# Three scans side by side: outputs and new states taken one unit later, side products moved behind the second products of each level, states updated from the bank in blocks

## The chip, the cores and the metric

One core of one Trainium2 chip. The time is the device time of one execution in microseconds, the median of three runs. All data are float32.

## The reference, cut to what matters

Two layers of a hybrid model over 256 context tokens and 256 latent tokens of width 1024. In each layer the normed tokens are projected, and the columns feed three groups of recurrences, each run forwards and backwards in chunks: a state space model (SSD, 8 heads, state 128), a gated linear recurrence (HGRN2, 4 heads of 64) and a gated delta rule (GDN, 4 heads of 64). Then come an output projection and a mixture of 64 experts. Only the recurrences are touched:

```python
# SSD:   h_t = exp(da_t) h_{t-1} + B_t (x_t dt_t)^T,         y_t = h_t C_t
# HGRN2: S_t = diag(f_t) S_{t-1} + k_t v_t^T,                o_t = S_t^T q_t
# GDN:   M_t = exp(g_t) (I - b_t k_t k_t^T) M_{t-1} + b_t k_t v_t^T,   o_t = M_t^T q_t
# GDN by chunk:
lhs = a_strict + jnp.eye(CHUNK)
sol = lax.linalg.triangular_solve(lhs, rhs, left_side=True, lower=True, unit_diagonal=True)
v_new = u_c - w_c @ s
o = qg_c @ s + qk_c @ v_new
s = d_c * s + ke_c^T @ v_new
```

Every latent scan starts from the last context state of its direction. In layer 1 the context tokens' outputs are not needed any more, only their states.

## The kernel before, in words

**Stages.** Per layer: norms, input projection, convolutions, then the scans, then output projection and experts (weights of 1 MB blocks stream in). The scans work on chunks of 128 tokens, four of them (two of context, two latent), in two directions: eight units (`UNITS`), alternating between the directions. A unit is live (`wanted` in the code) when its chunk's outputs are needed: all eight in layer 0, the last four in layer 1. `outs(l, u)` counts live units up to u. The first unit that visits a chunk (`SEEN`) writes the outputs `yraw`, the second adds to them.

**The chain in a unit.** The delta rule's triangular system is inverted by doubling in seven levels (j = 0 to 6), for four heads in two halves. At each level PE waits for a masked matrix from GpSimd (`masked`, line 643, semaphore `nt_ready`) and for the inverse so far from VectorE (`t_ready`), and makes the level's *first products* (4 matmuls, semaphore `p_ps`). ScalarE copies them out of the bank (line 807, `p_sb`). Then PE makes the level's *second products* with them (8 matmuls, at the last level 4, `q_ps`), and VectorE subtracts them from the inverse (`w_next`, through the helper at line 1064). Level 0 has first products only (`w_first`). A float32 matmul stands in the trace as two matmul records.

**The rest of the work in a unit** is placed by hand between these steps, in four in-order queues:
- PE: `decays` (cumulative decays as products with a triangle), `key_products`, `h_products` (HGRN's products of levels, four steps of 8 matmuls), the products with the delta state (`gks_ps`), and for the unit before `values` (new values of the delta rule), `ssd_outputs` and `ends` (delta outputs and new states).
- VectorE: for the unit before `hgrn_state`, `ssd_out`, `gdn_end`, `ssd_state`; for this one `gdn_rhs` (right-hand side), the HGRN keys at the chunk's end (`kend`), `h_levels` (masked copies of the level products out of the bank, its drain at line 1342 raises `h_cp`), score weighting of SSD, `hgrn_out`; for the next one `hgrn_scans`, `hgrn_levels`, `keys` and `queries` (line 1292; their drains at lines 1299 and 1304 raise `at_ready`). The drain at line 1385 ends `ssd_state`. Most operations are followed by a drain.
- ScalarE: the copies of first products, `levels_exp` (absolute value and exponential of 1792 columns, for HGRN's levels, semaphore `hexp`), `vn_copy` (the new values), the exponential of the space model's decays, decay steps (line 933).
- GpSimd: the seven masks of a unit, the products of HGRN's level factors with keys and queries (line 651), SSD's weighted inputs `xw` and `xdt`, the delta keys `kw`.

**Placement before.** PE puts `values` and `ssd_outputs` of the unit before between levels 0 and 1, `ends` after level 1's second products. Decays and key products of the next unit stand between the first and second products of levels 2 and 3; the last two steps of `h_products` stand between those of levels 4 and 5, behind a wait for `h_cp`; HGRN's output and new state between those of level 6. A state update of HGRN or of the delta rule multiplies the bank by a block mask `bd` into `tmp` and then does one scalar_tensor_tensor for each of two tiles of 128 columns; SSD's state is scaled in one operation and added to in another.

Of the kernel before, what the change touches and what calls it, by code (L numbers as in the profile page):

```python
# [147 lines left out]
def build(nc, A, out, scratch):  # L148
    f_dram, acc_dram, acc_odd, tab_dram = scratch
    with ExitStack() as ctx:  # L150
# [184 lines left out]
        for name, n in (  # L335
# [17 lines left out]
            ("ke_ps", U - 2), ("ke_sb", U - 2), ("ho_ps", U), ("hgrn_done", U),  # L353
            ("ssd_pre", U), ("e_ssd", U), ("cb_ps", U), ("att_ready", U), ("kw_ready", U), ("ssd_ps", U), ("ssd_sb", 2 * U),
# [235 lines left out]
        def _(pool):  # L590
# [36 lines left out]
            for l in range(DEPTH):  # L627
# [32 lines left out]
                for u, (i, d, c) in enumerate(UNITS):  # L660
                    wanted, un = c in LIVE[l], outs(l, u)
                    if wanted:
                        if u:
# [19 lines left out]
                    if wanted:  # L683
                        do(G.tensor_tensor(by_head(xdt[:, :]), xs(c), heads(dt_[:, c, d, 0:HS]), ALU.mult))
                    pool.drain().then_inc(S["kw_ready"], 1)
                    masked(u, 5)
                    masked(u, 6)
                    if u + 1 < U:
# [106 lines left out]
        def _(act):  # L795
# [41 lines left out]
            for l in range(DEPTH):  # L837
# [84 lines left out]
                def levels_exp(u):  # L922
                    wait("b_ready", u + 1, l)
                    if UNITS[u][2] in LIVE[l]:
                        f(e7[:, :, :], e7[:, :, :], ACT.Abs)
                        f(e7[:, :, :], e7[:, :, :], ACT.Exp, scale=-1.0)
# [13 lines left out]
                def vn_copy(u):  # L940
                    wait("vn_ps", u + 1, l)
                    f(vn[:, :], ps[:, 4, 0:HW], ACT.Identity, "vn_sb")
# [3 lines left out]
                levels_exp(0)  # L946
                e_gdn(0)
                for u, (i, _, c) in enumerate(UNITS):
                    wanted, un = c in LIVE[l], outs(l, u)
                    if u:  # L950
                        vn_copy(u - 1)
                        wait("ho_ps", u, l)
# [4 lines left out]
                    for j in range(1, LEVELS):  # L957
# [5 lines left out]
                        if j == 2:  # L963
# [3 lines left out]
                            if u + 1 < U:  # L967
                                e_gdn(u + 1)
                        if j == 5:
                            if wanted:  # L970
                                wait("ssd_pre", un, l)
                                f(E[:, :, :].rearrange("p h t -> p (h t)"), bank(6, 2), ACT.Exp, "e_ssd")
                            if i < NT - 1:
                                wait("ke_ps", u + 1, l)
                                f(kendT[:, :], ps[:, 5, 0:2 * P], ACT.Identity, "ke_sb")
                    if u + 1 < U:
                        levels_exp(u + 1)
# [74 lines left out]
        def _(dve):  # L1052
# [91 lines left out]
            for l in range(DEPTH):  # L1144
# [199 lines left out]
                def hgrn_out(u):  # L1344
                    _, _, c = UNITS[u]
                    if c in live:
                        wait("ho_ps", u + 1, l)
# [5 lines left out]

                def hgrn_state(u):
                    i, d, _ = UNITS[u]
                    if i < NT - 1:
                        wait("ho_ps", u + 1, l)
# [20 lines left out]
                def ssd_state(u):  # L1378
                    i, d, c = UNITS[u]
                    if i < NT - 1:  # L1380
                        wait("go_ps", u + 1, l)
                        sv = Ss[:, d, :, :].rearrange("p g f -> p (g f)")
                        tt(by_head(sv), by_head(sv), heads(etot[:, c, d, 0:HS]), ALU.mult)
                        tt(sv, sv, ps[:, 7, :], ALU.add)
                    dve.drain().then_inc(S["ssd_sb"], 1)

                def gdn_rhs(u):
# [3 lines left out]
                    h4 = lambda ap: ap.rearrange("p (h v) -> p h v", h=HH)  # L1391
                    tt(h4(rr[:, :]), h4(ps[:, 4, 0:HW]), gdn(eacs[:, c, d, HS:NDEC]), ALU.mult)
                    o = yraw[:, c, SW + HW:DM]
                    if c in live:
# [791 lines left out]
```

## Time and profile before

| | us |
|---|---|
| median of three runs | 2959.13 |
| lowest and highest | 2950.36, 2961.5 |
| the profiled execution | 2956.34 |
| its span | 2954.6 |
| mean granted TensorE clock | 0.917 of full |

| engine | busy us | share of the span | instructions |
|---|---|---|---|
| PE (matmul) | 2497.5 | 85% | 14732 |
| DVE (VectorE) | 1199.4 | 41% | 2349 |
| ACT (ScalarE) | 631.6 | 21% | 1140 |
| POOL (GpSimd) | 667.9 | 23% | 686 |

The shares are averages over stages with different limits. The scans fill about 323 to 717 us (layer 0) and 1890 to 2195 us (layer 1) of the span. Rows of the trace name an engine, the line of kernel.py (often that of a helper), the tile written and those read, and how long the engine stood idle before it and what ended that. `R` is the big scratch tile, `ring` holds a part of the working tiles during the scans, `ps` is the eight banks of PSUM. "DVEq" is a signal of VectorE's queue (a drain or a semaphore instruction) rather than of one of its operations.

### The profile page before, as it was taken

How to read it: one execution, taken by the hardware profiler on the slowest of the kernel's cores; microseconds unless marked ns; L12 is line 12 of the kernel's file. 1: busy time of each engine (PE TensorE's matmuls, PEld its weight loads, DVE VectorE, ACT ScalarE, POOL GpSimd, SP SyncE). 2: the span in 40 equal slices, each digit the busy share in tenths (PEclk: the TensorE clock that was granted, in tenths of full speed). 3: DMA queues.
4: the chain of work that ended last, by engine and by line, in shares of the span. 5: the costliest groups of instructions: out<-in, count | busy, mean ns of one | idle time of the engine just before them, and what ended most of it. 6: DMA issues, size and time to landing. Idle time of an engine off the chain costs nothing.

```text
span 2954.6 us, 43826 instructions
## 1 busy us (share of the span) xinstructions
PE 2497.5 (85%) x14732; PEld 1683.9 (57%) x14733; DVE 1199.4 (41%) x2349; ACT 631.6 (21%) x1140; POOL 667.9 (23%) x686
## 2 busy tenths in 40 slices
PE   5999788886866989999997598898867798999995
PEld 2348677776733555555554245787766455555552
DVE  4532576766261222222221543477664222222223
ACT  1125332322010111111111114523230111111111
POOL 0000253532013222222221000235321222222221
PEclk8999788988878999999999799999788899999998
DMA  6634000001152999999996352200016499999994
GB/s 257 256 132 90 1 1 1 1 1 34 46 222 96 367 353 358 348 336 333 365 349 217 131 199 71 47 1 1 1 34 246 167 367 362 367 365 358 381 351 148
DMA packets 188878, 573.16 MB, mean 194 GB/s; under 512 B 56543, under 2 KB 99879, under 8 KB 149831
## 3 DMA queue, kind: packets, MB, share of 16 engines
q1 hardware_dynamic: 162150, 520.29, 47.2%
q0 software_dynamic: 26592, 51.11, 7.1%
q8 instruction: 81, 1.33, 0.2%
q14 instruction: 55, 0.44, 0.0%
HBM read 552.37 MB, written 53.53 MB: 205 GB/s over the span
## 4 chain that ended last, share of the span: by engine, by line
PE 61%; DVE 13%; DMA 13%; issue 6%; ACT 2%; DVEq 2%; POOLq 1%; another core or an unknown queue 1%; ACTq 1%; SPq 1%; POOL 0%
PE ps L1659 56%; DMA featT<-ffn_rows,idx_in 7%; PE ps L1663 5%; DVE R L1064 4%; DMA R<-in_exp_down 4%; DVE featT L1064 1%; ACT R L807 1%; DVE R L1337 1%; DVE ring L1064 1%; POOLq L723 1%; DMA R<-in_w_mod 1%; ACT L807 1%; DMA R<-ffn_sum_even 1%; DVEq L1061 1%
## 5 line engine op out<-in xcount | busy, mean ns | idle before, releaser
L1659 PE MATMUL ps<-R 128*64 128x256 f32 (+5 forms) x9040 | 1427.7, 385 | 112.1 <-issue 49.4
L1659 PEld LDWEIGHTS ps<-R 128*64 128x64 f32 (+2 forms) x9040 | 884.7, 168 | 521.9 <-issue 284.7
L807 ACT ACTIVATE R<-ps 128x256 f32<-128x256 f32 (+3 forms) x395 | 175.4, 444 | 1197.9 <-PE ps L1659 1052.5
L1064 DVE TENSOR_TENSOR R<-R,ps 128x256 f32<-128x256 f32 (+2 forms) x250 | 137.3, 549 | 564.1 <-ACT R L807 500.4
L1659 PE MATMUL ps<-featT,ring 128*128 128x512 f32 (+1 forms) x768 | 312.4, 564 | 1.1 <-ACT R L807 0.8
L1659 PE MATMUL ps<-ring,R 128*128 128x128 f32 (+2 forms) x1200 | 262.4, 355 | 35.9 <-DMA ring<-in_sh_down 20.1
L1659 PEld LDWEIGHTS ps<-ring,R 128*128 128x128 f32 x1200 | 209.3, 215 | 70.4 <-issue 47.0
L1663 PE MATMUL ps<-ident,featT 128*128 128x128 f32 x1120 | 163.3, 292 | 98.3 <-DMA featT<-ffn_rows,idx_in 59.6
L1659 PEld LDWEIGHTS ps<-featT,ring 128*128 128x128 f32 x768 | 147.9, 196 | 162.8 <-issue 156.1
L643 POOL TENSOR_TENSOR R<-ring,lev 128x512 f32<-128x512 f32 x56 | 73.9, 1319 | 680.6 <-DVEq L1299 292.9
L1067 DVE TENSOR_SCALAR R<-ps,idx_out 128x512 f32<-128x512 f32 x128 | 96.1, 751 | 300.4 <-PE ps L1659 300.4
L1663 PEld LDWEIGHTS ps<-ident,featT 128*128 128x128 f32 x1120 | 128.8, 148 | 154.3 <-issue 64.6
L747 POOL DMA_INDIRECT ffn_sum_even<-R,idx_out x64 | 93.8, 1466 | 499.8 <-issue 499.8
L1073 DVE COPY R<-ps 128x256 f32<-128x256 f32 (+2 forms) x282 | 154.5, 548 | 112.5 <-PE ps L1663 91.3
L747 POOL DMA_INDIRECT ffn_sum_odd<-R,idx_out x64 | 94.2, 1472 | 439.0 <-issue 439.0
L807 ACT ACTIVATE R<-ps,idx_out 128x512 f32<-128x512 f32 x128 | 88.0, 688 | 380.0 <-PE ps L1659 380.0
L716 POOL DMA_INDIRECT featT<-ffn_rows,idx_in x128 | 126.8, 991 | 54.3 <-issue 49.8
L1002 ACT ACTIVATE R<-ps 128x512 f32<-128x512 f32 x128 | 76.4, 597 | 234.0 <-PE ps L1663 228.3
L1064 DVE TENSOR_TENSOR R<-R 128x256 f32<-128x256 f32 (+5 forms) x116 | 95.2, 821 | 66.0 <-ACT R L807 56.6
L1659 PE MATMUL ps<-ring,featT 128*128 128x256 f32 x512 | 113.7, 382 | 1.0 <-issue 1.0
L643 POOL TENSOR_TENSOR R<-R,lev 128x512 f32<-128x512 f32 x56 | 75.2, 1343 | 164.9 <-PE ps L1659 153.3
L1659 PEld LDWEIGHTS ps<-ring,featT 128*128 128x128 f32 x512 | 97.8, 192 | 17.0 <-issue 4.0
(197 smaller groups left out, 1837.6 us busy)
## 6 DMA issues: line engine op xcount, KB each, us to landing
R<-in_exp_gate SPq DMA_DIRECT2D x128, 1024.0 KB
R<-in_exp_up SPq DMA_DIRECT2D x128, 1024.0 KB
R<-in_exp_down SPq DMA_DIRECT2D x128, 1024.0 KB
R<-in_w_mod SPq DMA_DIRECT2D x48, 1024.0 KB, 7.4
ring<-in_w_in SPq DMA_DIRECT2D x30, 1024.0 KB, 5.4
ring<-in_w_out SPq DMA_DIRECT2D x8, 1024.0 KB, 7.5
ffn_sum_odd<-zero SPq DMA_DIRECT2D x6, 512.0 KB, 8.4
ffn_rows<-X SPq DMA_DIRECT2D x6, 512.0 KB
```

The source lines that it names most:

```text
L643: do(G.tensor_tensor(NTm[:, run % 2, :, :], AT[u % 2][:, :, :], lev[:, UNITS[u][1], j, :].unsqueeze(1).to_broadcast([P, HH, P]), ALU.mult) ...
L716: pool.indirect_dma_start(xg[s][0:n, :], None, f_dram, bass.IndirectOffsetOnAxis(idxG[s][0:n, 0:1].bitcast(U32), 0), bounds_check=TOK - 1, ...
L723: wide = pool.value_load(more[0:1, at_], min_val=0, max_val=1)
L747: pool.indirect_dma_start((acc_dram, acc_odd)[s % 2], bass.IndirectOffsetOnAxis(idxS[s][0:n, 0:1].bitcast(U32), 0), oe[s % 2][0:n, :], Non ...
L807: do(C.activation(out_, in_, func, **kw), name)
L1002: do(C.activation(xgT[b][:, 0:4, :].rearrange("p k t -> p (k t)"), ps[:, 0, :], ACT.Identity), "xt_sb")
L1061: dve.drain()
L1064: do(V.tensor_tensor(out_, a, b, op), name)
L1067: do(V.tensor_scalar(out_, a, s1, s2, op0, *(() if op1 is None else (op1,))), name)
L1073: do(V.tensor_copy(out_, in_), name)
L1659: return MM(out_, lhsT, rhs, start=start, stop=stop)
L1663: return nc.tensor.transpose(out_, in_, ident[0:k, 0:k])
```

## The change

Semaphores `hs_ps` (HGRN's new state product) and `st_ps` (SSD's) are added, so that outputs and states signal apart. Where an order is changed, it is that of PE, VectorE, ScalarE and GpSimd; no DMA is added or moved. In PE's queue:
- level 0: after its products `values`, `h_state`, `ssd_scores` of the unit before; the values now go to bank 3.
- level 1: the products with the delta state wait for `hgrn_done` in place of `vn_sb`.
- level 2: `ssd_outputs` of the unit before between first and second products (it stood at level 0).
- level 3: next unit's decays between the products; then SSD's new state of the unit before (it was part of `ends`).
- level 4: key products of the next unit and step 2 of `h_products`, all behind the second products; level 5: step 3 and the eight SSD decays, likewise.
- level 6: transposes of `kend` between the products, HGRN's output `h_out` behind them.

```diff
 # GpSimd: xw after mask 6
-                    do(G.tensor_tensor(by_head(xw[:, :]), xs(c), heads(wdt[:, c, d, 0:HS]), ALU.mult))
...
                     masked(u, 6)
+                    if i < NT - 1:
+                        if u:
+                            wait("st_ps", u, l)
+                        do(G.tensor_tensor(by_head(xw[:, :]), xs(c), heads(wdt[:, c, d, 0:HS]), ALU.mult))
+                    pool.drain().then_inc(S["kw_ready"], 1)
 # ScalarE
                     if u:
                         vn_copy(u - 1)
-                        wait("ho_ps", u, l)
+                    levels_exp(u)
+                    if un > 1:
+                        wait("ho_ps", un - 1, l)
                     f(eb[:, :], bh[:, :], ACT.Exp, "eb_ready")
...
+                    if i < NT - 1:
+                        wait("ke_ps", u + 1, l)
+                        f(kendT[:, :], ps[:, 5, 0:2 * P], ACT.Identity, "ke_sb")
+                    if wanted:
+                        wait("ssd_pre", un, l)
+                        f(E[:, :, :].rearrange("p h t -> p (h t)"), bank(6, 2), ACT.Exp, "e_ssd")
                     if u + 1 < U:
-                        levels_exp(u + 1)
+                        levels_abs(u + 1)
 # VectorE: states
+                def add_blocks(state, keep, new):
+                    for t in range(2):
+                        for half in range(2):
+                            own = slice(half * HD, (half + 1) * HD)
+                            V.scalar_tensor_tensor(state[own, t, own], state[own, t, own], keep[own, t:t + 1],
+                                                   new[own, t * P + half * HD:t * P + (half + 1) * HD], ALU.mult, ALU.add)
...
-                        tt(tmp[:, 0:2 * P].rearrange("p (t v) -> p t v", t=2), ps[:, 5, 2 * P:4 * P].rearrange("p (t v) -> p t v", t=2),
-                           bd[:, :].unsqueeze(1).to_broadcast([P, 2, P]), ALU.mult)
-                        for t in range(2):
-                            V.scalar_tensor_tensor(Sh[:, d, t, :], Sh[:, d, t, :], hdec[:, t:t + 1], tmp[:, t * P:(t + 1) * P], ALU.mult, ALU.add)
+                        wait("hs_ps", u + 1, l)
+                        add_blocks(Sh[:, d, :, :], hdec[:, :], ps[:, 5, 2 * P:4 * P])
...
-                        tt(by_head(sv), by_head(sv), heads(etot[:, c, d, 0:HS]), ALU.mult)
-                        tt(sv, sv, ps[:, 7, :], ALU.add)
+                        for q in range(HS):
+                            own = slice(q * HD, (q + 1) * HD)
+                            V.scalar_tensor_tensor(sv[:, own], sv[:, own], etot[:, c, d, q:q + 1], ps[:, 7, own], ALU.mult, ALU.add)
...
+                def scores(u):
+                    _, d, c = UNITS[u]
+                    if c in live:
+                        wait("cb_ps", outs(l, u), l)
+                        wait("e_ssd", outs(l, u), l)
+                        g2 = ps[:, 6, 0:NG * P].rearrange("p (g t) -> p g t", g=NG)
+                        tt(g2, g2, tri[:, d, :].unsqueeze(1).to_broadcast([P, NG, P]), ALU.mult)
+                        e4 = E[:, :, :].rearrange("p (g r) t -> p g r t", g=NG)
+                        tt(e4, e4, g2.unsqueeze(2).to_broadcast([P, NG, HS // NG, P]), ALU.mult, "att_ready")
 # VectorE: right-hand side
-                    tt(h4(rr[:, :]), h4(ps[:, 4, 0:HW]), gdn(eacs[:, c, d, HS:NDEC]), ALU.mult)
...
-                        tt(h4(to), h4(ps[:, 4, HW:2 * HW]), gdn(eacs[:, c, d, HS:NDEC]), ALU.mult)
-                    r22 = rr[:, :].rearrange("p (a f) -> p a f", a=2)
-                    tt(r22, cv[:, 12:14, tk(c)], r22, ALU.subtract, "r_ready")
-                    if c in live and SEEN[c] != u:
-                        tt(o, o, tmp[:, 0:HW], ALU.add)
+                    for q in range(HH):
+                        own = slice(q * HD, (q + 1) * HD)
+                        by = eacs[:, c, d, HS + q:HS + q + 1]
+                        V.scalar_tensor_tensor(rr[:, own], ps[:, 4, own], by,
+                                               cv[:, 12 + q // 2, c * P + (q % 2) * HD:c * P + (q % 2 + 1) * HD], ALU.mult, ALU.subtract)
+                        if c in live and SEEN[c] != u:
+                            V.scalar_tensor_tensor(o[:, own], ps[:, 4, HW + q * HD:HW + (q + 1) * HD], by, o[:, own], ALU.mult, ALU.add)
 # PE: after the last unit
                 values(U - 1)
+                ssd_scores(U - 1)
+                ends(U - 1)
                 ssd_outputs(U - 1)
-                ends(U - 1)
```

The comment lines name the place of a hunk. `gdn_end` changes like `hgrn_state`, and `levels_abs` is the first operation of the old `levels_exp`.

VectorE's order in a unit before: `w_first`; `hgrn_state`, `ssd_out` of the unit before; `w_next` 1; `gdn_end` (before), `gdn_rhs`; `w_next` 2; `ssd_state` (before), `hdec`, `eb`, `kend`, scans of the next unit; then ahead of each `w_next` 3 to 6 a step of `h_levels` and some of the next unit's `hgrn_levels`, `keys` after `w_next` 3, `queries` after 4, score weighting and `hgrn_out` of the same unit ahead of `w_next` 6.

After: `w_first`; `hgrn_out`, `hgrn_state`, `scores` of the unit before; `w_next` 1; `gdn_end` (before), `gdn_rhs`, `kend`, `hdec`, `eb`; `w_next` 2; `ssd_out` (before), `h_levels` 0; `w_next` 3; `ssd_state` (before), the next unit's scans, `h_levels` 1, `hgrn_levels` 0 and 1; `w_next` 4; `keys`, `queries` (next), `h_levels` 2, `hgrn_levels` 2 and 3; `w_next` 5; `h_levels` 3, `hgrn_levels` 4 to 6; `w_next` 6.

## Rows read from the trace of the kernel before

**Rows 1.** The page's first line.

```profile
span 2954.6 us, 43826 instructions
```

**Rows 2.** Stretches: us; PE, PEld, DVE, ACT, POOL busy (instructions); PEclk, DMA share, GB/s.

```profile
323.28:716.70 393.42, 327.30 (x2520) 308.14 (x2519) 262.66 (x478) 113.67 (x242) 165.49 (x207) 0.86 0.02 7
617.50:667.30 49.80, 41.30 (x323) 39.05 (x322) 35.56 (x65) 14.72 (x32) 21.59 (x27) 0.86 0.01 1
1911.40:1938.30 26.90, 24.47 (x189) 22.17 (x188) 18.20 (x35) 8.13 (x22) 10.93 (x10) 1.00 0.01 2
1995.40:2194.80 199.40, 162.93 (x1262) 153.07 (x1261) 132.13 (x232) 59.47 (x124) 82.58 (x103) 0.87 0.04 13
```

**Rows 3.** Waits in layer 0's scans: who <- for whom: us, times, longest.

```profile
DVE ring L1064 <- PE ps L1659: 39.6, 28, 6.0
DVE R L1064 <- PE ps L1659: 39.3, 28, 5.9
...
PE ps L1659 <- DVEq L1342: 18.2, 12, 2.6
PE ps L1659 <- DVEq L1304: 14.8, 7, 2.1
...
PE ps L1663 <- DVEq L1342: 11.7, 6, 2.2
...
PE ps L1659 <- DVEq L1385: 9.3, 6, 1.9
DVE featT L1064 <- PE ps L1659: 6.8, 8, 1.5
...
DVE R L1292 <- PE ps L1659: 5.3, 4, 1.8
...
DVE featT L1073 <- PE ps L1659: 4.9, 4, 2.1
```

**Rows 4.** VectorE's operations by shape in layer 0's scans: count | busy, mean ns | idle before.

```profile
L1064 DVE TENSOR_TENSOR R<-R,ps 128x512 f32<-128x512 f32 x50 | 34.4, 687 | 34.5 <-PE ps L1659 32.1 <-issue 0.2
...
L1064 DVE TENSOR_TENSOR R<-R 128x256 f32<-128x256 f32 x24 | 17.7, 737 | 1.8
L1064 DVE TENSOR_TENSOR R<-R 128x1024 f32<-128x1024 f32 x8 | 12.6, 1580 | 0.7 <-issue 0.2
L1064 DVE TENSOR_TENSOR R<-R 128x512 f32<-128x512 f32 x6 | 8.9, 1489 | 0.6
...
L1064 DVE TENSOR_TENSOR featT<-featT,R 128x256 f32<-128x256 f32 x4 | 5.4, 1361 | 0.4
L1064 DVE TENSOR_TENSOR R<-ps,bd 128x256 f32<-128x256 f32 x12 | 5.1, 425 | 1.0
...
L1361 DVE SCALAR_TENSOR_TENSOR R<-R,hdec 128x128 f32<-128x128 f32 x12 | 4.9, 448 | 0.4
```

**Rows 5.** Timeline of VectorE in unit 6 (start us, us, engine, line).

```profile
648.38 1.13 DVE L1292 SCALAR_TENSOR_TENSOR R<-ps,R,X 128x128 f32<-128x128 f32 x4 [1.80 <-PE ps L1659]
```

**Rows 6.** Timeline of ScalarE at the head of unit 6.

```profile
617.83 3.95 ACT L807 ACTIVATE R<-R 128x1792 f32<-128x1792 f32 x3
621.86 0.38 ACT L807 ACTIVATE R<-ps 128x256 f32<-128x256 f32 x1
...
622.82 1.28 ACT L933 ACTIVATE ring<-past_,R 128x128 f32<-128x128 f32 x4
```

**Rows 7.** Timeline of PE in unit 6.

```profile
619.81 1.06 PE L1659 MATMUL ps<-ident,R 128*128 128x128 f32 x8
620.70 3.72 PE L1659 MATMUL ps<-R 128*128 128x64 f32 x28
...
626.10 0.39 PE L1659 MATMUL ps<-R,ring 128*128 128x128 f32 x2
...
650.79 1.11 PE L1659 MATMUL ps<-R 64*128 64x64 f32 x16 [1.44 <-DVEq L1342]
```

**Rows 8.** Timeline of GpSimd at the head of unit 6.

```profile
621.96 3.34 POOL L651 TENSOR_TENSOR R<-R 128x128 f32<-128x128 f32 x7 [1.38 <-ACT R L807]
```

More of the change, by code:

```diff
@@ L966, in _ @@
                             act.drain().then_inc(S["m_ready"], 1)
[L967 to L975, printed above, removed]
+                        if j == 3 and u + 1 < U:
+                            e_gdn(u + 1)
+                    if i < NT - 1:
[4 more added lines that the diff above has]
+                        f(E[:, :, :].rearrange("p h t -> p (h t)"), bank(6, 2), ACT.Exp, "e_ssd")
                     if u + 1 < U:
-                        levels_exp(u + 1)
+                        levels_abs(u + 1)
                 vn_copy(U - 1)
@@ L1346, in hgrn_out @@
                     if c in live:
-                        wait("ho_ps", u + 1, l)
+                        wait("ho_ps", outs(l, u), l)
                         o = yraw[:, c, SW:SW + HW]
@@ L1424, in _ @@
                     if u:
+                        hgrn_out(u - 1)
                         hgrn_state(u - 1)
-                        ssd_out(u - 1)
+                        scores(u - 1)
                     w_next(u, 1)
@@ L1437, in _ @@
                         tt(eb[:, :].rearrange("p (t s) -> p t s", t=2), eb[:, :].rearrange("p (t s) -> p t s", t=2), hq[:, :, tk(c)], ALU.mult)
-                    wait("hexp", u + 1, l)
-                    tt(kend[:, :].rearrange("p (t s) -> p t s", t=2), e1[:, :].rearrange("p (t s) -> p t s", t=2), hk[:, d, :, tk(c)], ALU.mult, "kend_ready")
+                    dve.drain().then_inc(S["kend_ready"], 1)
+                    w_next(u, 2)
+                    if u:
+                        ssd_out(u - 1)
@@ L1440, in _ @@
+                    if wanted:
+                        h_levels(u, 0)
+                    w_next(u, 3)
+                    if u:
+                        ssd_state(u - 1)
                     if more_:
                         hgrn_scans(u + 1)
[L1442 to L1460 removed]
@@ new lines, in _ @@
+                    if wanted:
+                        h_levels(u, 1)
+                    if more_:
+                        hgrn_levels(u + 1, (0, 1))
+                    w_next(u, 4)
+                    if more_:
+                        keys(u + 1)
+                        queries(u + 1)
+                    if wanted:
+                        h_levels(u, 2)
+                    if more_:
+                        hgrn_levels(u + 1, (2, 3))
+                    w_next(u, 5)
+                    if wanted:
+                        h_levels(u, 3)
@@ L1461, in _ @@
+                    if more_:
+                        hgrn_levels(u + 1, (4, 5, 6))
+                    w_next(u, 6)
+                hgrn_out(U - 1)
                 hgrn_state(U - 1)
+                scores(U - 1)
+                gdn_end(U - 1)
                 ssd_out(U - 1)
-                gdn_end(U - 1)
                 ssd_state(U - 1)
@@ L1902, in _ @@
                             ins.then_inc(S["gks_ps"], 1)
-                        if j == 2 and more_:
+                            if u:
+                                wait("vn_sb", u, l)
+                        if j == 2 and u:
+                            ssd_outputs(u - 1)
+                        if j == 3 and more_:
                             wait("at_ready", 2 * u + 2, l)
@@ L1951, in _ @@
                                 h_products(u, 1)
+                        if j == 4:
                             if more_:
                                 wait("e_gdn", u + 2, l)
+                                if u:
+                                    wait("ssd_sb", 2 * u, l)
+                                key_products(u + 1, 0)
                                 key_products(u + 1, 1).then_inc(S["pre_ps"], 1)
-                        if j == 4 and wanted:
+                            if wanted:
+                                wait("h_cp", (un - 1) * 4 + 2, l)
+                                h_products(u, 2)
+                        if j == 5 and wanted:
+                            wait("h_cp", (un - 1) * 4 + 3, l)
+                            h_products(u, 3)
                             wait("m_ready", 3 + 2 * u, l)
@@ L1958, in _ @@
                             decays(u, Ms, HS, 6).then_inc(S["ssd_pre"], 1)
[L1959 to L1972 removed]
+                        if j == 6:
+                            h_out(u)
                 values(U - 1)
+                ssd_scores(U - 1)
+                ends(U - 1)
                 ssd_outputs(U - 1)
[L1975 removed]
                 wait("gdn_done", U, l)
```

147 lines of the change are left out of this document (66 added, 81 removed).

## The prediction

> **What bounds the kernel now.** I read the page first [rows 1]: one profiled execution, span 2954.6 us, 2956.3 us with what lies around it. The change touches only the scans, so I cut those out with a table of stretches [rows 2]: layer 0's eight units take 393.4 us, layer 1's four live ones 199.4 us, so a live unit takes 49 to 50 us and there are twelve; a unit whose outputs nobody wants takes 26.9 us (layer 1 has four). Units are nearly alike, so one is worked through (unit 6 of layer 0, 49.8 us) and multiplied.
>
> No engine is full there. In unit 6 PE is busy 41.3 of 49.8 us at a mean granted clock of 0.86 [rows 2]. The clock has two levels, so 0.86 means 28% of the unit, 14 us, at 1.2 GHz; at 2.4 GHz throughout, the same products would take about 41.3 x 0.86 = 35.5 us. VectorE is busy 35.6 us. The view of waits over layer 0 says who holds whom [rows 3]: DVE waits for PE 39.6 + 39.3 + 6.8 + 5.3 + 4.9 = 95.9 us, 12.0 us per unit; PE waits for DVE's signals 18.2 + 11.7 us (line 1342, the end of a copy of HGRN's level products), 14.8 us (line 1304, the queries) and 9.3 us (line 1385, the space model's state): 54 us, 6.7 per unit. Two engines that work in order hold each other up in turn: the bound is a chain through both, with both queues nearly full. Without its waits DVE would need (393.4 - 95.9) / 8 = 37.2 us per unit, PE 35.5.
>
> Why PE waits can be read in the code: line 1342's signal is waited for ahead of the level's second products (levels 4 and 5, and the key transposes of level 6), so the inverse stands still for a side job.
>
> **Part 1: VectorE's work.** Price of the new small operations first. The trace has no 64-column scalar_tensor_tensor. Four of 128 columns that read a bank end 1.13 us after the first began [rows 5]; at some 0.34 us each that is one every 0.26 us, and 64 columns less at 0.96 GHz (67 ns, the slope between DVE's 256 columns at 425 ns and 512 at 687 ns gives 65 ns [rows 4]) makes 0.20 us. Bounds: half of 0.26, 0.13, and a whole 128-column operation unshortened, 0.34. I take 0.20. By part, for an average unit (gaps of about 0.08 us between drained operations counted):
> - the delta rule's right-hand side: two operations of 425 ns and one of 737 ns, on second visits (half of the units) an addition of 1361 ns [rows 4], with gaps 1.85 and 3.3 us; after, four small ones and one of 425 ns, or eight small ones: 1.3 and 1.7. Mean -1.05.
> - states of HGRN and delta rule: each one operation of 425 ns and two of 448 ns [rows 4] with gaps, 1.4; after, four small, 0.85. Both: -1.1, in six units of eight.
> - the space model's state: 1489 + 687 ns [rows 4] and gaps, 2.3; after, eight small and a drain, 1.7: -0.6, in six of eight.
> - score weighting: 1580 ns with both inputs in SBUF [rows 4]; after, one input is the bank, so twice the 512-column bank row less a fixed part, 1.22: -0.35.
>
> Sum: -1.05 - 0.75 x 1.7 - 0.35 = -2.7 us per unit. There are 18 small operations in an average unit, so the bounds of their price make it -4.0 and -0.1 us. DVE: 37.2 - 2.7 = 34.5 us.
>
> What speaks against this part is a rule of the Trainium skill, "VectorE: DVE Perf Modes", section on the TRN2 errata: each operation pays its latency anew, so tile at 512 elements or more. Its formula for fp32, (N + 151) / 0.96 ns, gives 424 ns at 256 columns, as the trace has it, and an estimate of 0.224 us at 64. With that the part would bring -2.3 us, some 5 us less over the kernel. The rule counts the fixed cost alone; the rows [rows 4] show that what is replaced costs more than its columns (512 columns 1489 ns from SBUF, 687 ns with a bank).
>
> **Part 2: order.** I walk through one live unit, t from the first product of level 0, all at 2.4 GHz. A group of 8 product records takes 0.9 us (level 0's start 619.81, the next group 620.70), 28 records with the four wide ones 3.6 us, and a step of HGRN's level products, 16 short records, I put at 1.1 us [rows 7].
> - Head. PE: level 0 (0.9), values (1.8), HGRN's state and the scores (2.65), level 1's products (3.55). They used to be followed by the space outputs; now these come at level 2. ACT is the new tail: it used to raise the levels' exponentials (3.95 us) ahead of the values' copy [rows 6] and now does the exponential behind it: copy 0.4, 1792 columns 1.7 (half of the 3.95 us, less the small one in it), two of 256 columns 0.9, four decay steps 1.3, gaps 0.3, from t = 2.0 to 6.6. Only then does it copy level 1's products: 2nd products of level 1 from t = 7.1. Before it was 626.10 - 619.81 = 6.3 [rows 7]. **That costs 0.8 us** and leaves PE idle 2.6 us and DVE 2.3 us (it has its scores done at 5.9 and wants level 1 at 8.2).
> - GpSimd is behind the same exponential: its multiplication by the keys began at 621.96, 2.15 us after level 0 [rows 8], now at 4.8; 3.3 us for it and 1.3 for a mask make level 2's mask 9.8. PE wants it at 10.4, behind the ends: hidden by 0.6 us; if the cover goes, it costs 1 us.
> - Level 2: DVE waits 0.9 for the ends (10.6), then delta rule's end, right-hand side, key work: 15.7; level-2 update to 17.2. PE: ends 10.4, level 2 with space outputs between its products 15.8, HGRN's level step 16.9.
> - Level 3: PE waits 1.0 for the space output (18.8), decays, second products 21.5, new state 22.5, level step 23.6. DVE: space output, copy, update to 23.0.
> - Level 4: DVE state 24.8, scans, copy, differences 27.8, update 29.3; PE 29.7. Level 5: DVE keys and queries 31.9, copy, differences, update 35.5; PE waits 0.5 for a copy, then step and eight decays: 36.1. Level 6 with transposes and HGRN's output at the end: 39.8.
>
> So at full clock a unit takes 39.8 us, with DVE waiting 4.0 (2.3 + 0.9 + 0.85 at the next level 0). Waits for line 1342 are mostly gone, since copy and second products now overlap; queries have a whole level for cover; the space state's signal is wanted only after level 4's second products. Then the clock: it cost up to 5.8 us of PE time per unit; PE will be fuller, and the unwanted unit, busy 24.5 of 26.9 us, had 1.00 [rows 2]. But the hole of the head remains, and I leave 3.5 us. DVE's waits: 7.5 instead of 12.0.
>
> **Sum.** 34.5 + 7.5 = 42.0 us per live unit against 49.2: -7.2, twelve times: -86 us. Each layer's tail grows, because scores, ends, then space outputs now follow one another behind the last values with no level beside them (a weighting of 1.6 and a group of 0.4): +2 each, +4. The four unwanted units are full of PE already: 0, from -1 to +1 each. Later stages only move earlier. 2956.3 - 82 = 2874 us; the median of the runs is 2.8 above the profiled one, so 2875 to 2877. I say 2876.
>
> **Rivals.**
> - *Waits only move* (ACT's late copies, GpSimd's mask, PE's wait for the space output make up for those removed): DVE still waits 12 us. For it: the head got 0.8 us longer by my walk. Against: 54 us of PE's waits are on three named signals, all of which get cover. -2.7 x 12 + 4 = -28: 2928.
> - *Nothing comes of it*: that, and small operations at 0.34 us: -0.1 x 12 + 4: 2959. The change would not do what it says. Needs both.
> - *Slower by the clock*: with 4.6 us idle a unit bound by PE takes 40.1 us plus half of its time at 1.2 GHz. The clock fell, in the trace, in stretches behind PE's idle ones, and the head now has one of 2.6 us in every unit. It decides from 20.6 us at 1.2 GHz per unit (now 14): beyond it the kernel is over 0.5% slower. With 24 us: 52.1 a unit, 2.9 x 12 + 4: 2995. Against: PE's idle share falls otherwise.
> - *Clock held, small operations at 0.13*: 33.2 + 4.0: -12 x 12 + 4: 2816.
>
> **How the numbers follow.** Forecast 0.72, clock held 0.04, waits move 0.14, nothing 0.06, slower 0.04. No change is within 0.5%, 15 us, about what a measurement tells. The forecast case and its neighbours end below 2944, the second too: faster 0.90, same 0.06, slower 0.04. Range: from waits of 4 with half of the bounds (2840) up to the rival at 2928, taken in: 2840 to 2930.
>
> **What would show it.** After: layer 0's units at about 42 us; PE's waits on the copies of the level products under 10 us in the layer (30 before); granted clock over 0.9 in the units; small operations at 0.2 us; ACT's exponential directly behind the values' copy and PE idle some 2 us there; the right-hand side in under 2 us. I'd be wrong if the units stay at 46 us or more (waits moved), or if the clock is under 0.8.

## The result, and the profile after

The changed kernel takes 2859.7 us (median of four, 2854.3 to 2864.4) against 2960.3 us for the kernel before on the same chip: ratio 0.966, 95% interval 0.964 to 0.968, 100 us less. The forecast was 2876 us. The profiled execution has a span of 2862.6 us, 92.0 us shorter than that of before [rows 1]. Where those 92 us lie, a table of stretches shows, cut as [rows 2] are: layer 0's scans, unit 6 of them, layer 1's scans whole, and layer 1's four unwanted units. Columns: us; busy us (instructions) of PE, PEld, DVE, ACT, POOL; granted clock; DMA share; GB/s.

```profile
321.10:653.42 332.32, 290.35 (x2520) 270.26 (x2519) 258.74 (x550) 113.64 (x242) 156.44 (x205) 0.98 0.03 9
574.66:616.77 42.11, 37.18 (x331) 34.54 (x329) 34.32 (x75) 14.01 (x30) 19.00 (x25) 1.00 0.01 1
1827.98:2103.73 275.75, 240.81 (x1984) 222.48 (x1983) 195.16 (x441) 89.12 (x200) 118.34 (x137) 0.98 0.03 10
1827.98:1936.52 108.54, 96.04 (x735) 87.96 (x735) 71.72 (x175) 30.92 (x78) 43.32 (x38) 0.97 0.00 1
```

Layer 1's scans and their unwanted units before, from the same view of the kernel before:

```profile
1888.39:2194.88 306.49, 260.86 (x1984) 241.97 (x1983) 205.31 (x374) 89.13 (x200) 124.79 (x139) 0.90 0.03 9
1888.39:1997.12 108.73, 99.65 (x739) 90.63 (x739) 74.02 (x143) 31.30 (x78) 43.69 (x38) 0.97 0.00 1
```

Layer 0's scans went from 393.4 to 332.3 us (-61), layer 1's from 306.5 to 275.8 (-31), together all of the 92. The four unwanted units did not move. A live unit went from 49.2 to 41.5 us in layer 0. Two things stand out beside that: the granted clock rose from 0.86 to 0.98, and VectorE's busy time fell by only 3.9 us in layer 0 (262.7 to 258.7).

The waits in layer 0's scans, to be held against [rows 3]:

```profile
DVE R L1072 <- PE ps L1690: 20.0, 18, 2.5
...
DVE ring L1072 <- PE ps L1690: 12.9, 12, 3.9
PE ps L1690 <- DVEq L1350: 12.9, 12, 1.5
...
PE ps L1690 <- ACT R L811: 9.0, 7, 1.3
...
PE ps L1690 <- DVEq L1375: 5.2, 6, 0.9
DVE featT L1072 <- PE ps L1690: 5.0, 7, 0.9
```

VectorE's waits for PE fell from 95.9 us to 37.9, and two more rows of 1.0 us each. PE's for the end of a copy of level products (line 1342, now 1350) fell from 29.9 to 12.9; those for the queries (14.8) are gone. New is PE's wait for ScalarE, 9.0 us in seven units.

The head of unit 6, PE and then ScalarE:

```profile
566.26 1.11 PE L1690 MATMUL ps<-ident,R 128*128 128x128 f32 x8
567.31 2.05 PE L1690 MATMUL ps<-R 128*128 128x64 f32 x16
569.20 1.06 PE L1690 MATMUL ps<-ring,R 128*128 128x128 f32 x8
571.13 1.16 PE L1690 MATMUL ps<-R 128*128 128x128 f32 x8 [0.87 <-DVEq L1375]
573.58 0.46 PE L1690 MATMUL ps<-R,ring 128*128 128x128 f32 x2 [1.30 <-ACT R L811]
```

```profile
568.91 2.68 ACT L811 ACTIVATE R<-R 128x1792 f32<-128x1792 f32 x3
571.67 1.28 ACT L940 ACTIVATE ring<-past_,R 128x128 f32<-128x128 f32 x4
573.05 0.85 ACT L811 ACTIVATE R<-ps 128x256 f32<-128x256 f32 x2
```

PE starts level 1's second products 7.3 us after level 0, where it was 6.3 us [rows 7]: they need ScalarE's copies of the first products (573.05), and ScalarE does the exponential and the decay steps before those.

VectorE by shape, layer 0's scans, against [rows 4] (count | busy, mean ns):

```profile
L1289 DVE TENSOR_TENSOR R<-R 128x256 f32<-128x256 f32 x49 | 28.0, 618 | 3.9 <-issue 3.9
...
L1072 DVE TENSOR_TENSOR featT<-featT,R 128x512 f32<-128x512 f32 x8 | 11.0, 1370 | 0.7
L1072 DVE TENSOR_TENSOR R<-R,ps 128x1024 f32<-128x1024 f32 x8 | 9.8, 1222 | 0.6
L1398 DVE SCALAR_TENSOR_TENSOR R<-R,ps 128x64 f32<-128x64 f32 x48 | 9.7, 276 | 1.0 <-PE ps L1690 0.6
...
L1367 DVE SCALAR_TENSOR_TENSOR R<-R,ps 64x64 f32<-64x64 f32 x24 | 6.7, 280 | 0.7
...
L1081 DVE COPY hdec<-R 128x2 f32<-128x2 f32 x8 | 5.3, 660 | 0.6
```

Three of these are operations that the change did not touch. The same three before:

```profile
L1281 DVE TENSOR_TENSOR R<-R 128x256 f32<-128x256 f32 x49 | 20.4, 453 | 5.0 <-issue 5.0
...
L1064 DVE TENSOR_TENSOR featT<-featT,R 128x512 f32<-128x512 f32 x8 | 6.7, 841 | 0.7
...
L1073 DVE COPY hdec<-R 128x2 f32<-128x2 f32 x8 | 2.3, 290 | 1.3 <-issue 1.2
```

They grew by 7.6 + 4.3 + 3.0 = 14.9 us. What made them grow is taken up below, with e5.

### The profile page after: what moved, and what is told of

Its sections match the earlier page's. It is cut to its first block, busy times and chain, and to the rows that moved or that the text cites. A ratio compares the mean times of both kernels' runs of the same rounds, so it can differ in the third digit from the quotient of the medians.

```text
span 2862.6 us, 43941 instructions
## 1 busy us (share of the span) xinstructions
PE 2441.5 (85%) x14732; PEld 1630.0 (57%) x14733; DVE 1185.9 (41%) x2489; ACT 631.5 (22%) x1140; POOL 652.5 (23%) x682
## 4 chain that ended last, share of the span: by engine, by line
PE 57%; DVE 15%; DMA 14%; issue 5%; ACT 3%; DVEq 2%; POOLq 1%; ACTq 1%; SPq 1%; another core or an unknown queue 0%; POOL 0%
PE ps L1690 52%; DMA featT<-ffn_rows,idx_in 7%; DMA R<-in_exp_down 5%; PE ps L1694 5%; DVE R L1072 3%; ACT R L811 2%; DVE featT L1072 2%; DVE ring L1072 1%; DVE R L1345 1%; DVEq L1069 1%; DMA R<-in_w_mod 1%; POOLq L727 1%; ACT L811 1%; DMA R<-ffn_sum_even 1%; DVE R L1075 1%
## 5 line engine op out<-in xcount | busy, mean ns | idle before, releaser
L1690 PE MATMUL ps<-R 128*64 128x256 f32 (+6 forms) x9040 | 1395.3, 380 | 100.5 <-issue 44.5
L1690 PEld LDWEIGHTS ps<-R 128*64 128x64 f32 (+2 forms) x9040 | 854.0, 162 | 511.0 <-issue 289.0
L1072 DVE TENSOR_TENSOR R<-R,ps 128x256 f32<-128x256 f32 (+2 forms) x250 | 143.7, 575 | 548.6 <-ACT R L811 492.4
L1690 PE MATMUL ps<-ring,R 128*128 128x128 f32 (+2 forms) x1200 | 245.7, 337 | 30.3 <-DMA ring<-in_sh_down 18.9
L1690 PEld LDWEIGHTS ps<-ring,R 128*128 128x128 f32 x1200 | 193.4, 197 | 64.5 <-issue 44.7
L1694 PE MATMUL ps<-ident,X 128*128 128x128 f32 (+1 forms) x114 | 25.7, 409 | 82.7 <-DVE X L1075 62.2
```

Source lines behind the costliest of these rows:

```text
L1072: do(V.tensor_tensor(out_, a, b, op), name)
L1690: return MM(out_, lhsT, rhs, start=start, stop=stop)
L1694: return nc.tensor.transpose(out_, in_, ident[0:k, 0:k])
```

## The experiments

Twelve kernels were run, each timed against the kernel before on its own chip. "Scans" below are the stretches of layer 0 and of layer 1 in the profiled execution, cut like those above (393.5 and 306.5 us before, 332.3 and 275.8 changed). e1 and e2 are not in the table, for the reason given with them.

| run | time us | ratio to before, 95% | scans, layer 0 / 1 |
|---|---|---|---|
| changed | 2859.7 | 0.966 (0.964 to 0.968) | 332.3 / 275.8 |
| e3 steps ahead | 2934.8 | 0.992 (0.990 to 0.995) | 382.7 / 302.5 |
| e4 clock held | 2928.7 | 0.990 (0.986 to 0.993) | 378.6 / 299.1 |
| e5 order only | 2873.8 | 0.971 (0.969 to 0.973) | 339.5 / 283.9 |
| e6 arithmetic only | 2947.1 | 0.996 (0.994 to 0.997) | 393.2 / 299.1 |
| e7 steps behind | 2903.2 | 0.981 (0.979 to 0.982) | 358.8 / 290.0 |
| e8 decay steps later | 2841.0 | 0.960 (0.958 to 0.963) | 318.6 / 268.9 |
| e9 block order | 2856.1 | 0.967 (0.964 to 0.969) | 332.2 / 276.5 |
| e10 decays first | 2849.8 | 0.965 (0.963 to 0.967) | 325.5 / 276.0 |
| e11 exponential first | 2844.0 | 0.963 (0.961 to 0.965) | 327.0 / 273.1 |
| e12 four edits | 2831.3 | 0.957 (0.955 to 0.959) | 313.5 / 263.1 |

My theory: the order made most of the gain, by taking PE's waits out of the chain, and VectorE's small operations a smaller, separate part. Rivals: the small operations carry it; or the clock does.

**Order without arithmetic (e1, e5).** The changed kernel with the old operations:

```diff
-                        add_blocks(Sh[:, d, :, :], hdec[:, :], ps[:, 5, 2 * P:4 * P])
+                        tt(tmp[:, 0:2 * P].rearrange("p (t v) -> p t v", t=2), ps[:, 5, 2 * P:4 * P].rearrange("p (t v) -> p t v", t=2),
+                           bd[:, :].unsqueeze(1).to_broadcast([P, 2, P]), ALU.mult)
...
-                            V.scalar_tensor_tensor(sv[:, own], sv[:, own], etot[:, c, d, q:q + 1], ps[:, 7, own], ALU.mult, ALU.add)
+                        tt(by_head(sv), by_head(sv), heads(etot[:, c, d, 0:HS]), ALU.mult)
+                        tt(sv, sv, ps[:, 7, :], ALU.add)
```

> The changed kernel with VectorE's old operations (states through the block mask, space state in two 512-column operations, right-hand side in 256-column ones, score weights through tmp); all orders as changed. Theory (most of the 100 us is order, VectorE's small operations save about 2.4 us a live unit and VectorE is nearly the bound in the new order): about 2885 us, 2875 to 2900. Rival (the small operations carry the gain): 2915 or more. Rival (they save nothing, or the fixed cost of each eats it up): 2862 or less.

The changed right-hand side has the opposite sign, and ScalarE's copy of the new values turns it back (scale -1). e1 left that copy as changed beside the old right-hand side, and e2 the old copy beside the new one, so the delta rule's new values have the other sign, the tokens are routed otherwise, and the path for experts with over 128 tokens runs as well. Their times (3333 and 3401 us) therefore say nothing of the scans; the scans' own stretch has no operation that depends on the data and can be read: 340.5 us. e5 is the same with the sign matched:

> Order alone again, with the sign of the new values matched to the old right-hand side (e1 had it unmatched). In e1 the scans of layer 0, whose operations do not depend on the data, took 340.5 us (393.5 before, 332.3 changed). Theory: the same here, layer 1 in proportion (four live units: 4 us more than changed), 2860 + 8 + 4 = 2872 us, 2865 to 2880. Rival (my price of 2.4 us a live unit for the small operations): 2885.

Measured 2873.8 us, layer 0's scans 339.5: 54 of the 61 us of layer 0 come with the order alone. The arithmetic on top is worth 7.2 us there, 0.9 us a unit, and 14 us in the medians of all.

**Arithmetic without order (e2, e6).** The kernel before with the new operations (the reverse of the edit above).

> The kernel before with the new VectorE operations alone, order as before. Theory (the engines wait for each other, so work taken off VectorE comes back only in part): 1 to 2.5 us a live unit, 2930 to 2950 us. Rival (small operations carry the gain): 2900 to 2915. Rival (nothing): 2955 or more.

The stretch in e2: 390.1 us. With the sign matched:

> Arithmetic alone again, sign matched (e2 had it unmatched; layer 0's scans took 390.1 us there). Theory: with the old order the time taken off VectorE turns into waits for PE: -3.4 and -1.7 us, 2950 to 2957 us, not to be told from the kernel before. Rival (small operations carry a part of their own): 2935 or less.

Measured 2947.1 us, 0.4% less than before, 3 us below what I expected and clear of zero, but small. Layer 0's scans stay at 393.2; layer 1's fell by 7.4 us, to 299.1, all of it in the live units, and no run says why the two layers differ. In layer 0 PE's waits for line 1342 rose from 29.9 to 39.4 us:

```profile
PE ps L1663 <- DVEq L1342: 27.4, 18, 2.9
PE ps L1663 <- DVEq L1304: 14.8, 7, 2.1
PE ps L1667 <- DVEq L1342: 12.0, 6, 2.2
```

In layer 0, work taken off VectorE did not shorten the chain: its own waits for PE grew as well (the first two of [rows 3] from 78.9 to 82.2 us).

**One place in PE's queue (e3, e7).** In the changed kernel, HGRN's level steps 2 and 3 back between first and second products:

```diff
+                        if j in (4, 5) and wanted:
+                            wait("h_cp", (un - 1) * 4 + j - 2, l)
+                            h_products(u, j - 2)
                         for hf in range(2) if j else ():
                             wait("p_sb", 2 * (u * (LEVELS - 1) + j - 1) + hf + 1, l)
...
-                                h_products(u, 2)
...
-                            h_products(u, 3)
```

> The changed kernel with steps 2 and 3 of HGRN's level products put back between first and second products of levels 4 and 5, behind their wait. Theory (that place is what held PE up): 2 to 4 us a live unit, 2885 to 2905 us, and PE's waits on the copies' drain go from 13 to over 30 us in layer 0. Rival (VectorE is full and PE's place in the level does not matter): within 5 us of the changed kernel's 2860.

It cost 75 us, more than twice the middle of what I expected: layer 0's scans 382.7, PE's waits for the copies 45.2 us, the granted clock 0.91 instead of 0.98. Unit 5 shows how. PE:

```profile
529.50 1.27 PE L1690 MATMUL ps<-R 64*128 64x64 f32 x16 [3.29 <-DVEq L1350]
539.60 1.26 PE L1690 MATMUL ps<-R 64*128 64x64 f32 x16 [2.71 <-DVEq L1350]
```

and VectorE right behind it:

```profile
532.81 0.69 DVE L1072 TENSOR_TENSOR ring<-ring,ps 128x512 f32<-128x512 f32 x1 [2.52 <-PE ps L1690]
534.21 0.69 DVE L1072 TENSOR_TENSOR ring<-ring,ps 128x512 f32<-128x512 f32 x1 [0.71 <-PE ps L1690]
535.92 1.13 DVE L1300 SCALAR_TENSOR_TENSOR R<-ps,R,X 128x128 f32<-128x128 f32 x4 [1.02 <-PE ps L1690]
```

PE waits 3.3 us for VectorE's copy, so its second products come late; then VectorE has nothing to do for 2.5 us, since its next operation needs them. Here one misplaced wait is paid twice, once on each engine. The reverse, in the kernel before:

```diff
-                        if j in (4, 5) and wanted:
-                            wait("h_cp", (un - 1) * 4 + j - 2, l)
-                            h_products(u, j - 2)
...
+                        if j in (4, 5) and wanted:
+                            wait("h_cp", (un - 1) * 4 + j - 2, l)
+                            h_products(u, j - 2)
                         if j == 4 and wanted:
                             wait("m_ready", 3 + 2 * u, l)
```

> The kernel before with one thing changed: steps 2 and 3 of HGRN's level products behind the second products of levels 4 and 5 in place of ahead of them. e3, the reverse in the changed kernel, cost 75 us. Theory (this place is the largest single part of the order, and it works by itself): layer 0's scans 355 to 375 us, the kernel 2905 to 2935 us. Rival (it pays only with the rest of the order, since the queries' wait behind it remains): layer 0's scans over 380 us, the kernel over 2940 us.

Measured 2903.2 us, just under my band, layer 0's scans 358.8, within it. This one move gives 57 us by itself, where the whole change gives 100, and 35 where it gives 61 in layer 0. The clock went from 0.86 to 0.90 with it, so what it is worth has the clock's part in it, like e3's 75 us.

**The clock (e4).** The kernel before with idle products ahead of PE's waits:

```diff
+                def fill(n, b):
+                    for _ in range(n):
+                        mm(ps[:, b, 2 * P:3 * P], ident[:, :], ident[:, :])
...
                         if j in (4, 5) and wanted:
+                            fill(6 if j == 4 else 2, 0)
                             wait("h_cp", (un - 1) * 4 + j - 2, l)
```

and four more such places (4, 4, 8 and 8 products).

> The kernel before with 32 idle products a live unit (128x128, written to a free part of a bank and read by nobody) placed ahead of PE's waits, some 7 us a unit at full clock, to hold the clock. Theory (the higher granted clock of the changed kernel is mostly a consequence): clock in layer 0's scans over 0.95 and 2930 to 2965 us. Rival (the clock made most of the gain, up to 5.8 us a live unit): 2890 to 2905 us.

```profile
322.56:701.17 378.61, 351.82 (x3024) 334.99 (x3023) 266.08 (x479) 113.67 (x242) 167.24 (x207) 0.96 0.02 8
```

Clock 0.96, layer 0's scans 14.9 us shorter, the kernel 28 us (2928.7, just under my band). So in the old order holding the clock is worth some 15 us in layer 0, or more, since the fillers themselves may cost a part of it. With the clock at 0.96, against 0.98 in the changed kernel, 46 of the 61 us are still missing; the clock alone did not bring them here. Its share can't be added to the order's, since the clock also rose with the order alone (e5: 0.97, without fillers). What it is worth in the new order was not run.

**The head and ScalarE (e8, e11).** The changed kernel, decay steps behind the copies of level 1:

```diff
-                    if u + 1 < U:
-                        steps(Mg, u + 1, range(HS, NDEC))
-                    act.drain().then_inc(S["m_ready"], 1)
...
+                        if j == 1:
+                            if u + 1 < U:
+                                steps(Mg, u + 1, range(HS, NDEC))
+                            act.drain().then_inc(S["m_ready"], 1)
```

> The changed kernel with ScalarE's four decay steps of the next unit (1.3 us) behind its copies of level 1's first products in place of ahead of them. Theory (the head of a live unit waits for ScalarE: exponential behind the values' copy, decay steps, then the copies): layer 0's scans 8 x 1.0 to 1.3 us shorter, PE's wait for ScalarE from 9.0 to under 3 us, the kernel 2843 to 2850 us. Rival (GpSimd's mask of level 2, behind the same exponential, takes the place at once): less than 4 us gained.

Measured 2841.0 us, 2 us under my band, layer 0's scans 318.6, 1.7 us a unit and more than the steps' own 1.3; PE's wait for ScalarE 1.1 us where it was 9.0. The theory holds for the wait; where the gain beyond 1.3 comes from isn't shown. A wait for GpSimd's masks, the rival, came in its place, but with 3.8 us in all it is small. PE's second products of level 1 now start 5.9 us after level 0:

```profile
551.56 1.11 PE L1691 MATMUL ps<-ident,R 128*128 128x128 f32 x8
...
557.50 0.46 PE L1691 MATMUL ps<-R,ring 128*128 128x128 f32 x2
```

And the exponential ahead of the values' copy again, the order of before:

```diff
                         vn_copy(u - 1)
-                    levels_exp(u)
...
                         levels_abs(u + 1)
+                        levels_exp(u + 1)
```

> The changed kernel with ScalarE's exponential back ahead of the values' copy (absolute value and exponential together at the end of the unit, as before the change). Theory (in the head ScalarE is full from the values' copy to level 1's copies, so it saves the 0.5 us that it stands idle between the absolute value and the values; GpSimd starts 1 to 2 us earlier): 0 to 1 us a live unit faster, 2848 to 2860 us. Rival (the values' copy behind the exponential delays the ends and all after them): 5 us or more slower.

Measured 2844.0 us, 4 us under my band, but the kernel before was faster on that chip too. The ratios, 0.963 (0.961 to 0.965) and 0.966 (0.964 to 0.968), overlap a little; the scans are 5.3 and 2.7 us shorter and PE's wait for ScalarE 6.0 us instead of 9.0. This part of the change probably cost a little.

**Is VectorE the bound now? (e10, e9)**

```diff
-                            wait("h_cp", (un - 1) * 4 + 3, l)
-                            h_products(u, 3)
                             wait("m_ready", 3 + 2 * u, l)
                             wait("at_ready", 2 * u + 4, l) if more_ else wait("ssd_sb", 2 * u, l)
                             decays(u, Ms, HS, 6).then_inc(S["ssd_pre"], 1)
+                            wait("h_cp", (un - 1) * 4 + 3, l)
+                            h_products(u, 3)
```

> The changed kernel with level 5's eight decays ahead of step 3 of HGRN's level products, so that PE does not stand 1.27 us before that step. Theory (from level 2 on VectorE's queue is the bound, with no wait before its updates of levels 3 to 6; PE's waits there cost nothing): within 4 us of the changed kernel, while PE's waits for line 1350 fall from 12.9 to about 6 us in layer 0. Rival (both engines are the bound): 10 us or more faster.

The ratio, 0.965, can't be told from the changed kernel's 0.966 (the medians are 10 us apart, but the kernel before was 7.6 us faster on that chip, too); PE's waits for line 1350 fell to 8.3 us, not 6. That is my theory's side, yet not clean: layer 0's scans are 6.9 us shorter and layer 1's are not, and in layer 0 VectorE was busy 251.7 us, 7.1 less for the same operations. The level differences ahead of level 6 tell why. VectorE, then GpSimd, in the changed kernel, unit 6:

```profile
605.80 2.17 DVE L1289 TENSOR_TENSOR R<-R 128x256 f32<-128x256 f32 x3 [0.17 <-issue]
```

```profile
605.87 1.48 POOL L643 TENSOR_TENSOR R<-R,lev 128x512 f32<-128x512 f32 x1 [5.20 <-PE ps L1690]
```

and in e10:

```profile
596.49 1.55 DVE L1289 TENSOR_TENSOR R<-R 128x256 f32<-128x256 f32 x3 [0.17 <-issue]
```

```profile
595.81 1.28 POOL L643 TENSOR_TENSOR R<-R,lev 128x512 f32<-128x512 f32 x1 [4.48 <-PE ps L1690]
```

The three differences take 2.17 us where a GpSimd mask starts right beside them, and 1.55 where it ends (597.09) 0.6 us into them. Over the whole of layer 0's scans, GpSimd overlaps 21 of these 49 differences in the changed kernel and 9 in e10, and they are busy 28.0 and 23.5 us. VectorE's waits for PE, all counted, stayed (40.4 and 40.7 us). So what layer 0 gained in e10 lies in VectorE's busy time, most of it in that overlap, and not in the wait that PE was spared.

The block updates of a state by halves of the partitions:

```diff
-                    for t in range(2):
-                        for half in range(2):
+                    for half in range(2):
+                        for t in range(2):
```

> The changed kernel with the four block updates of a state in another order: both tiles of the upper 64 partitions, then both of the lower, in place of changing partitions each time. In the changed kernel these follow each other every 0.29 us (577.48, four in 1.16), 128-partition ones of the same width every 0.19. Theory (changing between the two halves of the partitions keeps two operations from overlapping): four in 0.96 us instead of 1.16, under 0.4 us a live unit, 2856 to 2860 us. Rival (64 partitions cost more in themselves): 1.16 us stays.

```profile
568.22 0.97 DVE L1367 SCALAR_TENSOR_TENSOR R<-R,hdec,ps 64x64 f32<-64x64 f32 x4
```

0.97 us for four where it was 1.16, as expected; the kernel's ratio is 0.967, the same as changed.

**Together (e12).** The edits of e8, e9, e10 and e11 in one kernel.

> The changed kernel with four edits together: decay steps of the next unit behind level 1's copies (e8), exponential ahead of the values' copy (e11), level 5's decays ahead of step 3 (e10), block updates by half (e9). Singly they took 13.7, 5.3, 6.9 and 0.1 us off the changed kernel's 332.3 us in layer 0's scans. Theory (e8 and e11 shorten the same stretch of ScalarE, so they add only in part; e10 works at another place): layer 0's scans 308 to 315 us, the kernel 2822 to 2838 us. Rival (with ScalarE out of the head, GpSimd's mask or the wait for HGRN's state takes its place at once): no better than e8, 2840 us.

Measured 2831.3 us, ratio 0.957 (0.955 to 0.959), layer 0's scans 313.5, both as expected: 28 us faster than the changed kernel by the medians, 125 faster than before. The rival had it no better than e8; it is 10 us faster by the medians, though the intervals of the ratios (0.957 and 0.960) overlap a little, and 5.1 and 5.8 us shorter in the two scans.

## Why the prediction was right, and where it wasn't

**The bound** was named rightly. PE's waits on VectorE's signals fell from 54.0 to 18.1 us in layer 0, and putting one of them back (e3) returned 75 us.

**Part 1, VectorE's work, was mis-sized.** I had 2.7 us less a live unit, 37.2 to 34.5. Taking the waits off, the changed kernel's VectorE needs (332.3 - 39.9) / 8 = 36.6 us; e5 against the changed kernel gives 0.9 us of time and (265.25 - 258.74) / 8 = 0.8 us of busy time. Two terms failed.
- The block updates: 0.29 us each, not 0.20, since they change between the halves of the partitions (e9); 0.20 held for the 128-partition ones (eight in 1.62 us). With six block updates in an average unit that is 0.5 us of the 1.8 missing. The states went from 5.1 + 4.9 + 5.9 us (block mask, lines 1361 and 1412) to 13.4, where I had counted on 6.6 us less.
- The prices of the removed operations, read in the old order. The order alone changed them, before anything was removed. e5, which still has them, in layer 0's scans:

```profile
L1289 DVE TENSOR_TENSOR R<-R 128x256 f32<-128x256 f32 x49 | 28.0, 618 | 4.0 <-issue 4.0
...
L1072 DVE TENSOR_TENSOR R<-R 128x1024 f32<-128x1024 f32 x8 | 10.0, 1248 | 0.6
L1072 DVE TENSOR_TENSOR featT<-featT,R 128x512 f32<-128x512 f32 x8 | 8.8, 1103 | 0.7
...
L1081 DVE COPY hdec<-R 128x2 f32<-128x2 f32 x8 | 6.6, 824 | 0.6
...
L1072 DVE TENSOR_TENSOR R<-R 128x512 f32<-128x512 f32 x6 | 4.2, 692 | 0.7 <-PE ps L1694 0.4
```

The six scalings of the space model's state take 692 ns there, where I had priced them at 1489, and the score weights 1248 where I had 1580 [rows 4]. The three untouched groups had already grown by 7.6 + 2.1 + 4.3 = 14.0 of the 14.9 us. So it was the new order that took time off the operations to be removed and put it on others; taking them out afterwards (e5 to the changed kernel) changed these three by 0.9 us in all. For the space model's state the new form even costs more in the new order: 9.7 us in small operations, where e5 has 4.2 us and six 512-column operations of 687 ns, 8.3 in all. In the old order (e6) a part did pass on with the removal: the level differences grew by 3.1 us and the next unit's scans by 3.2, while VectorE's busy time fell by 4.2.

What lies behind it is GpSimd. The Trainium skill, "SBUF — State Buffer", section "SBUF: two separate sides", says that a VectorE operation with two SBUF inputs and a GpSimd operation that reads SBUF exclude each other for a whole instruction. The trace agrees: the 256-column level differences (`hgrn_levels`, line 1289) take 411 ns at least, 424 in the median and 1497 at most, and those with a bank as input keep to 687 ns at 512 columns in both kernels. Of the 49 differences in layer 0's scans, those that no GpSimd operation overlaps in time take 427 ns at most, in all fourteen kept traces; those that one does overlap take 880 ns on the mean in the changed kernel. There are 2 of the latter in the kernel before, 18 in e5, 21 in the changed kernel and 7 in e6. The copy to `hdec` has one input, so that sentence doesn't cover it, but it shows the same: in all kept traces 168 to 171 ns where no GpSimd operation overlaps it, and up to 1196 in the changed kernel otherwise.

The rule on small tiles that I weighed (the Trainium skill, "VectorE: DVE Perf Modes", section on the TRN2 errata) would have given an estimate of 0.224 us an operation; the 128-partition ones came every 0.19, below it, the 64-partition ones every 0.29, above it, because they change partitions each time (e9).

**Part 2, the order, was right in its mechanism and nearly in its size.** The walk through a unit gave 39.8 us; 42.1 were measured in unit 6, 41.5 on the mean. Level 1's second products were to start at t = 7.1: 7.3. GpSimd's mask of level 2 was to be hidden by 0.6 us: it ended at 575.9 and PE took it at 576.8. VectorE's waits were to be 4.0 us of the walk and 3.5 for the clock; they are 5.0. **The clock's allowance was mis-sized:** the clock went to 0.98 and the hole in the head (0.87 + 1.30 us) did not bring it down.

So 42.0 us a unit was right as a sum of two errors of about 2 us, opposite in sign: VectorE's work 36.6 instead of 34.5, its waits 5.0 instead of 7.5. That they cancelled is luck. The walk could have warned me: its 39.8 us with 4.0 of waiting hold 35.8 us of VectorE's work, not 34.5, and with 35.8 + 7.5 I would have said 2892. The lower end of the range doesn't follow either: 34.5 + 4.0 us a unit is 2835 before any bound of the price is used, not 2840. The tails grew by 2.9 and 2.5 us, 2 each forecast; the unwanted units moved by 0.2 us in all, 0 forecast. The forecast sum, 82 us, stands against 92 in the profiled executions: the twelve live units, with the tails, came out 0.8 us better than said, each. The medians differ by 100, since the profiled execution of the kernel before was 4 us faster than its median and that of the changed kernel 5 us slower than its own.

**The rivals.** *Waits only move* was wrong except for ScalarE's 9.0 us, which was on my list and is real: e8 took it out and gained 19 us. *Slower by the clock* was wrong; the clock followed PE's filling. What I had not seen is how much hangs on one move: e7 alone gives 57 us, and I had spread the gain over all of them.

**Signs given.** Clock over 0.9: yes. Units at 42: yes. Waits for the copies under 10 us: 12.9. Right-hand side under 2 us: 578.76 to 580.4, yes. ScalarE's exponential right behind the values' copy: yes (568.45 and 568.91). PE idle some 2 us there: 0.87 + 1.30. Small operations at 0.2: only those over all partitions.

## What to carry to other kernels

Where two in-order engines pass work back and forth, look first at what each one waits for *ahead of* the product that the other needs next: a side job's wait there is paid on both engines, and moving it behind that product gave 57 us here (e7), where all savings of instructions gave 14. Price an operation that you remove at its shortest time in the trace as well as at its mean, above all when the order changes too: what it loses beside another engine depends on what runs next to it, and in a new order others lose it. And a move that opens a chain shows its new tail in the same profile (here ScalarE ahead of level 1's copies): reading it again gave another 28 us, 19 of them by that one move (e8).

## What the runs showed of the hardware that I had not expected

- Four scalar_tensor_tensor of 64 columns on 64 partitions take 1.16 us when they change between lower and upper partitions each time, 0.97 us when they change once; the recorded length of one is 279 to 280 ns (median) in both. Eight on all 128 partitions take 1.62 us.
- Idle products, 7 us of them a unit, made a kernel faster (e4: 28 us) by holding the granted clock at 0.96 instead of 0.86.
- A run of three VectorE subtractions of 256 columns (the level differences) took 1.55 or 2.17 us, with the same operations, depending on when GpSimd's mask began. A change of order alone raised the number of differences that meet a GpSimd operation from 2 to 18 of 49 (e5), and VectorE's time for them from 20.4 to 28.0 us.
